# Rotary partners fetched by transfers, the layer norm's sums two chunks sooner, the delta gates on GpSimd, and two row turns held to norms

## The chip, the core and the metric

The kernel runs on one core of a Trainium2 chip. A core has a matmul engine (TensorE, PE in the profile), a vector engine (VectorE, DVE), an activation engine (ScalarE, ACT), a general engine (GpSimd, POOL) and one that here only issues transfers (SyncE, SP); each works through its own list of instructions and waits for the others by semaphores. They share the on-chip memory SBUF; matmuls write to PSUM, eight banks of 2 KB a partition. The metric is device time in microseconds (us) of one launch.

## The reference

Everything is fp32, 256 tokens, width 1024. Two blocks follow one another. Block one has two hybrid layers; block two (norms modulated by a condition vector, latent attention beside a Hyena convolution, SwiGLU) is touched here by one row turn only. Cut to what the change meets:

```python
def hybrid_layer(x, ...):                    # twice
    h = rms_norm(x, norm_w)
    aq, ak, av, az, c_glu, cz, dq, dk, dv, dz, db, da, gates = split(h @ w_in)
    # diff attention: 8 heads, two 64-wide halves each
    q, k = apply_rope(aq), apply_rope(ak)    # [t1*cos - t2*sin, t2*cos + t1*sin]
    p = softmax(q k^T / 8 + causal);  a = p[0] - lam * p[1];  y_a = (rms(a v) * silu(az)) @ w_o
    # conformer convolution
    u = causal_conv31(a_half * sigmoid(g_half)) + b
    y_c = (silu(layer_norm(u)) * silu(cz)) @ w_conv_out
    # gated delta rule: 8 heads of 128, chunks of 64 tokens
    q, k, v = silu(causal_conv4([dq, dk, dv]));  q, k = l2_normalize(q), l2_normalize(k)
    beta = sigmoid(db);  g = -exp(a_log) * softplus(da + dt_bias);  g = cumsum(g)
    y_d = (rms(delta_rule(q, k, v, g, beta)) * silu(dz)) @ w_dn_out
    return x + (s_a * y_a + s_c * y_c + s_d * y_d) @ w_out      # s = sigmoid(gates)
```

apply_rope needs, for each row d of a 64-wide half, its partner row 32 further up or down, once with the sign turned. softplus is worked out as max(a, 0) + ln(1 + exp(−|a|)), with a correction of the logarithm for the rounding of 1 + exp(−|a|).

## The kernel before

Activations lie transposed: 128 channels on the partitions, 256 tokens along a row. Weights come as 128x128 tiles in the order of use, 16 to a load of 1 MB, which SyncE issues into a ring of four. Precision is kept by splitting: ScalarE writes the rounded high part of a load (L778), GpSimd the rest (L663, or VectorE where it has time), and TensorE makes three products for each tile, high by high, low by high, high by low (L1948 to L1950). One output tile of 128 channels over 1024 inputs is a "chunk": 8 tiles, 24 products into one of four PSUM banks (pg), which another engine drains. The other four banks (ps) hold everything that isn't a weight product: norms, rotations, scores.

The order of chunks is written out by a function and is the same for all engines. For a layer of block one: ag (16), qk (16), v (8, tokens on the partitions), dn (24, the delta rule's q, k and v before their convolution), cz 0 to 3 with the narrow projection for beta and the decay (BA) between, then the attention loop of 18 steps, into which cz 4 to 7 and c_out 0 to 15 are spread as fillings, then the delta rule, the three output projections with their gates, and w_out. From the order follow tables that the engines share: after which drain a tile may be read, and how far ahead of a chunk its high and low parts are made.

What the change touches, with the lines of the profile. TensorE rotates the pairs of q and k tiles by a constant matrix (rot, L2123): four of the eight behind v3 and v5, four ahead of dn1, dn2, dn5 and dn6; VectorE's rope (L1656 to L1660) multiplies by the tables. VectorE adds the last three taps of the short convolution for each dn chunk (sconv, L1428), with taps of the 31-wide one (L1413) between. The layer norm's channel sum is made by VectorE (L1723) after sconv 16 and 17, added over the partitions by TensorE (L2359) ahead of dn20; ScalarE squares the centered rows after dn23, VectorE sums them (L1731) and TensorE adds them (L2185) ahead of cz1. For the delta gates ScalarE makes exp and ln, VectorE the eight operations of delta_log (L1493 to L1501) in step 0 of the attention loop, TensorE the running sums (L2206) in step 1, VectorE the rest in step 2. GpSimd multiplies cz 4 to 7 into the branch (L689 to L691). PE L2013 is a row turn: a row of modulation values that block two needs is brought onto the partitions. PE L2149 are attention scores, L2179 a head norm's sums.

```python
for part in range(4):                              # TensorE, v
    for tt in range(NT):
        tokens_first("v", l, 2 * part + tt, ...)
    if part in (1, 2):
        rot1(2 * part - 2); rot1(2 * part - 1)
for i in range(24):                                # TensorE, dn
    if i in (1, 2, 5, 6): rot1(ROPES_V + (1, 2, 5, 6).index(i))
    if i in DQ_AT: half_norm(...)                  # DQ_AT = (15, 18)
    if i == LN_MEAN:
        pe.wait_ge(sem("ln_added"), l + 1)         # the mean's matmul
    chunk("dn", l, i, KD, hx, T)
```

## Time and profile before

| | us |
|---|---|
| three runs | 2552.84, 2544.14, 2553.32 |
| median | 2552.84 |
| profiled execution | 2549.82 |
| its span, first to last instruction | 2548.0 |
| TensorE busy | 2484.7 |
| GpSimd, ScalarE, VectorE busy | 1455.7, 1246.3, 1171.3 |

The profile is of one execution. Its mean granted clock of TensorE was 0.993 of full speed. Times of the timeline are from the span's start; in a row, the first number is the start, the second how long the instruction (or the run of xN alike) took, and in brackets stands how long the engine was idle ahead of it and what ended that. Matmuls are pipelined: a product of 256 columns is shown with 0.28 us, but the next one begins 0.12 us later. In the program's names HH and HL are the high and low parts of the normed input, X holds the convolution branch, big the attention's and the delta rule's tiles, ba the delta gates.

### The profile page before, as it was taken

What the parts mean: (1) busy time and instruction counts of PE and PEld (TensorE: products, weight loads), DVE (VectorE), ACT (ScalarE), POOL (GpSimd) and SP (SyncE); (2) the same over time, 40 slices, a digit from 0 to 9 for tenths busy, and PEclk for the clock granted to TensorE, in tenths of its full rate; (3) what the DMA queues carried; (4) which work ended last, traced back from release to release, by engine and by line L of the source; (5) the groups of instructions that cost most, each with busy time, mean ns of one, the idle gap of its engine ahead of it and who ended that gap; (6) DMA issues with size and microseconds to landing.
All of it is one profiled execution on the core that took longest, in us unless ns stands there. A gap on an engine that the chain in (4) does not pass through costs nothing.

```text
span 2548.0 us, 42067 instructions
## 1 busy us (share of the span) xinstructions
PE 2484.7 (98%) x16588; PEld 2170.4 (85%) x16588; DVE 1171.3 (46%) x2176; ACT 1246.3 (49%) x2113; POOL 1455.7 (57%) x835
## 2 busy tenths in 40 slices
PE   7998999999999899999999999999999999999998
PEld 7997989888999788898777877778888878898998
DVE  8896645444878645536415613331101123535144
ACT  6467654355546764436544522443323345636543
POOL 6875746456977664544533343646565546464970
PEclk9999999999999899999999999999999999999999
DMA  6543343345544344335421022232222233235554
GB/s 244 180 167 145 133 166 134 139 175 182 182 173 160 131 156 154 121 137 206 175 83 66 34 83 81 89 116 90 92 99 95 88 116 127 82 140 193 188 182 149
DMA packets 50601, 347.63 MB, mean 136 GB/s; under 512 B 5361, under 2 KB 8689, under 8 KB 8945
## 3 DMA queue, kind: packets, MB, share of 16 engines
q1 hardware_dynamic: 47840, 340.31, 37.1%
q10 hardware_dynamic: 2576, 4.72, 0.6%
q8 instruction: 133, 2.18, 0.3%
q14 instruction: 52, 0.42, 0.1%
HBM read 343.96 MB, written 1.05 MB: 135 GB/s over the span
## 4 chain that ended last, share of the span: by engine, by line
PE 91%; DVE 4%; ACT 3%; issue 1%; POOL 1%; DMA 1%; ACTq 0%; DVEq 0%; SPq 0%; POOLq 0%
PE pg L1948 23%; PE pg L1950 23%; PE pg L1949 23%; PE ps L2266 2%; PE pg L1971 2%; PE ps L2287 2%; PE ps L2285 1%; PE ps L2423 1%; PE ps L2404 1%; PE ps L2117 1%; ACT ring_hi L778 1%; PE ps L2123 1%; PE ps L2092 1%; PE ps L2504 1%; PE ps L2497 1%
## 5 line engine op out<-in xcount | busy, mean ns | idle before, releaser
L663 POOL TENSOR_TENSOR ring_lo<-ring,ring_hi 128x1024 fp32r<-128x1024 f32 (+3 forms) x502 | 1169.9, 2345 | 705.8 <-ACT ring_hi L778 704.8
L1948 PE MATMUL pg<-HH,ring_hi 128*128 128x256 f32 (+1 forms) x3264 | 1038.7, 318 | 8.1 <-POOL ring_lo L663 5.9
L1949 PE MATMUL pg<-HH,ring_lo 128*128 128x256 f32 (+1 forms) x3264 | 992.2, 304 | 0.0
L1950 PE MATMUL pg<-HL,ring_hi 128*128 128x256 f32 (+1 forms) x3008 | 920.0, 306 | 0.0
L1948 PEld LDWEIGHTS pg<-HH,ring_hi 128*128 128x128 f32 x3264 | 619.2, 190 | 73.8 <-issue 36.9
L1949 PEld LDWEIGHTS pg<-HH,ring_lo 128*128 128x128 f32 x3264 | 619.4, 190 | 43.4 <-issue 16.5
L1950 PEld LDWEIGHTS pg<-HL,ring_hi 128*128 128x128 f32 x3008 | 570.5, 190 | 28.3
L778 ACT ACTIVATE ring_hi<-ring 128x1024 fp32r<-128x1024 f32 (+3 forms) x572 | 563.8, 1003 | 30.3 <-DMA ring<-in_w_stream_dram 22.3
L788 ACT ACTIVATE take<-pg 128x256 f32<-128x256 f32 (+1 forms) x242 | 103.7, 429 | 452.6 <-PE pg L1950 445.0
L1950 PE MATMUL pg<-big_r,ring_hi 128*128 128x256 f32 (+1 forms) x928 | 299.3, 323 | 0.0
L1948 PE MATMUL pg<-big_r,ring_hi 128*128 128x256 f32 (+1 forms) x752 | 246.0, 327 | 3.9 <-DVE ring_lo L1633 2.7
L1949 PE MATMUL pg<-big_r,ring_lo 128*128 128x256 f32 (+1 forms) x752 | 244.1, 325 | 0.0
L1900 DVE TENSOR_TENSOR big_r<-big,big_r 128x512 fp32r<-128x512 f32 (+1 forms) x44 | 58.8, 1336 | 362.7 <-ACT big_r L1253 362.7
L1950 PEld LDWEIGHTS pg<-big_r,ring_hi 128*128 128x128 f32 x928 | 174.5, 188 | 15.3
L1413 DVE SCALAR_TENSOR_TENSOR ps<-big,prm,ps 128x256 f32<-128x256 f32 x464 | 183.6, 489 | 0.0
L788 ACT ACTIVATE big<-pg 128x256 f32<-128x256 f32 (+1 forms) x136 | 59.3, 436 | 232.2 <-PE pg L1950 229.9
L1948 PEld LDWEIGHTS pg<-big_r,ring_hi 128*128 128x128 f32 x752 | 141.4, 188 | 21.2 <-DVE ring_lo L1633 3.3
L1949 PEld LDWEIGHTS pg<-big_r,ring_lo 128*128 128x128 f32 x752 | 141.7, 188 | 13.1 <-issue 0.2
L707 POOL TENSOR_TENSOR X<-X,take 128x256 f32<-128x256 f32 (+1 forms) x50 | 50.4, 1012 | 126.9 <-ACT take L1184 126.9
L1633 DVE TENSOR_TENSOR ring_lo<-ring,ring_hi 128x1024 fp32r<-128x1024 f32 (+3 forms) x70 | 79.8, 1175 | 43.1 <-ACT ring_hi L778 43.1
L1184 ACT ACTIVATE take<-pg,mod 128x256 f32<-128x256 f32 x58 | 25.1, 471 | 145.0 <-PE pg L1950 145.0
L1612 DVE TENSOR_TENSOR big<-big,ps 128x512 f32<-128x512 f32 x40 | 27.5, 688 | 136.8 <-PE ps L2287 136.8
(350 smaller groups left out, 3337.7 us busy)
## 6 DMA issues: line engine op xcount, KB each, us to landing
ring<-in_w_stream_dram SPq DMA_DIRECT2D x320, 1024.0 KB, 4.8
hn<-in_consts_dram ACTq DMA_DIRECT2D x2, 1024.0 KB, 6.0
cst<-in_consts_dram SPq DMA_DIRECT2D x1, 1472.0 KB, 19.5
prm<-in_params_dram SPq DMA_DIRECT2D x1, 1110.0 KB, 9.3
X<-in_xT_dram SPq DMA_DIRECT2D x1, 1024.0 KB, 5.8
X<-in_ctxT_dram ACTq DMA_DIRECT2D x1, 1024.0 KB, 5.9
out_dram<-H ACTq DMA_DIRECT2D x4, 256.0 KB, 2.2
cst<-in_consts_dram SPq DMA_DIRECT2D x1, 768.0 KB, 16.5
```

The source lines that it names most:

```text
L663: pool.tensor_tensor(ring_lo[:, slot, cols], ring[:, slot, cols], ring_hi[:, place * P:(place + n) * P].bitcast(F32), SUB).then_inc(sem(LO ...
L778: act.activation(ring_hi[:, place * P:(place + n) * P], ring[:, slot, cols], ACT.Copy)\
L788: act.activation(dst, ready(j)[:, 0:n], func, scale=scale).then_inc(sem("drained"), 1)
L1413: ins = dve.scalar_tensor_tensor(acc if t < CONV_K - 1 else CV[:, k, :], U[:, k, t:t + T], PR("conv_dw_w", w), acc, MUL, ADD)
L1633: dve.tensor_tensor(ring_lo[:, slot, cols], ring[:, slot, cols], ring_hi[:, place * P:(place + n) * P].bitcast(F32), SUB).then_inc(sem(LOW ...
L1900: dve.tensor_tensor(AFL[l][:, c, :], AF[l][:, c, :], AFH[l][:, c, :].bitcast(F32), SUB).then_inc(sem("af_low"), 1)
L1948: first = pe.matmul(out, a[0], b[0], start=start, stop=False)
L1949: pe.matmul(out, a[1], b[0], start=False, stop=False)
L1950: return first, pe.matmul(out, a[0], b[1], start=False, stop=stop)
L1971: ins = pe.matmul(pg[part, j % 4, :], sc[:, c, :], tile(4), start=c < MOD_TILES, stop=c >= k - MOD_TILES)
L2266: ins = pe.matmul(ps[:, 1, s], LM[v % 2][:, s], TM[:, s], start=True, stop=True)
L2287: ins = pe.matmul(ps[:, 2, s], XS[:, s], TT[:, s], start=True, stop=True)
```

## The change

1. The rotation matmuls of block one are gone. ScalarE issues four transfers from SBUF to SBUF of 32 partitions x 2048 floats (256 KB each) for the first half of the qk tiles after draining qk8, four for the second after v0; they bring the partner rows into two spare buffers. ScalarE then copies each pair of tiles (128x512) to the PSUM bank where the rotation's result stood: two copies after v3, two after v5, one each after dn1, 2, 5 and 6. The sign lies in the sine table.
2. LN_MEAN goes from 20 to 18, so that the mean's matmul stands ahead of dn18. The square is made ahead of dn22's copy and its sum on VectorE ahead of sconv 22, instead of both behind dn23.
3. delta_log is made by GpSimd, in nine operations of 128x16, right behind cz4's products; the reciprocal is replaced by exp(−ln) on ScalarE. The running sums become a chunk of their own ("decay") in a bank of pg in step 7 of the loop, drained by ScalarE, and VectorE's rest moves from step 2 to step 8.
4. The row turn of "do" 0 goes from layer 0's gates into the norm of layer 1, and that of norm 5 from ahead of a k chunk of block two into norm 6.

```diff
@@ -80 +74 @@
-    c["inv1"] = np.tile(inv1, 4)[:, None]
+    c["inv1"] = np.concatenate([-inv1, inv1, -inv1, inv1])[:, None]
@@ -173,0 +168 @@
+LATE_TURNS = {1: ("do", 0), 6: ("norm", 5)}
@@ -184 +179,6 @@
-    return {"before": [("part", x) for x in rows[:1]] * 2, "after": rows, "turns": [("modt", *x[1:]) for x in rows]}[side]
+    late = [("modt", *x) for x in MOD_AT.get(LATE_TURNS.get(i), [])]
+    turns = [] if ("norm", i) in LATE_TURNS.values() else [("modt", *x[1:]) for x in rows]
+    return {"before": [("part", x) for x in rows[:1]] * 2, "after": rows + late, "turns": turns}[side]
+DECAY_STEP = 7
@@ -188 +188,3 @@
-    return spread([("cz", l, m) for m in range(EARLY_CZ, KD)] + [("c_out", l, i) for i in range(2 * KD)], ATT_STEPS + LAG + 1)
+    fills = spread([("cz", l, m) for m in range(EARLY_CZ, KD)] + [("c_out", l, i) for i in range(2 * KD)], ATT_STEPS + LAG + 1)
+    fills[DECAY_STEP].append(("decay", l, 0))
+    return fills
@@ -235 +237 @@
-    return gates[:2] + [row] + gates[2:4] + [turn] + gates[4:]
+    return gates[:2] + [row] + gates[2:4] + ([turn] if l else []) + gates[4:]
@@ -533 +535,0 @@
-        GCS = ps[:, 3, 288:304].rearrange("p (c h) -> p c h", c=NT)
@@ -589 +591,2 @@
-        LN_MEAN = 20
+        LN_MEAN = 18
+        LN_SQUARE = 22
@@ -692,0 +696,12 @@
+            def delta_log(l):
+                pool.wait_ge(sem("over_abs"), l + 1)
+                link(pool.tensor_scalar(NGC, B1, 1.0, None, ADD))
+                link(pool.tensor_scalar(NGC, NGC, -1.0, None, ADD))
+                link(pool.tensor_tensor(NGC, B1, NGC, SUB))
+                link(pool.tensor_tensor(NGC, NGC, GC, MUL))
+                link(pool.tensor_tensor(B2, B2, NGC, ADD))
+                link(pool.tensor_scalar(B0, B0, 0.0, None, MAX))
+                link(pool.tensor_tensor(B0, B0, B2, ADD))
+                link(pool.tensor_tensor(B0, B0, rep(EXA, NT), MUL))
+                pool.tensor_scalar(G, B0, -1.0, None, MUL).then_inc(sem("g_done"), 1)
@@ -721,0 +737,2 @@
+                    if m == EARLY_CZ:
+                        delta_log(l)
@@ -898,0 +918,16 @@
+            def turn_qk(l, half):
+                act.wait_ge(sem("drained"), DRAINED["qk", l, 8 * half + 7])
+                for a, b in ((0, 32), (32, 0), (64, 96), (96, 64)):
+                    act.dma_start(QK_TURNED[half][a:a + 32, :], big[b:b + 32, 2048 * half:2048 * (half + 1)])\
+                        .then_inc(sem(f"qk_turned{half}"), 16)
+            def turned_to_psum(l, jj):
+                i = 8 * l + jj
+                act.wait_ge(sem(f"qk_turned{jj // 4}"), 64 * (l + 1))
+                if i >= 2:
+                    act.wait_ge(sem("rope"), i - 1)
+                act.activation(ps[:, 2 + i % 2, :], QK_TURNED[jj // 4][:, jj % 4 * 2 * T:(jj % 4 + 1) * 2 * T], ACT.Copy)\
+                    .then_inc(sem("turned"), 1)
@@ -966,0 +1002,2 @@
+                act.wait_ge(sem("ln_abs"), l + 1)
+                act.activation(GC, B2, ACT.Exp, scale=-1.0).then_inc(sem("over_abs"), 1)
@@ -969,2 +1006,3 @@
-                act.wait_ge(sem("gc_ready"), l + 1)
-                act.activation(BEG, GCS, ACT.Exp).then_inc(sem("exp_gc"), 1)
+                sums = ready(CHUNK["decay", l, 0])[:, 0:2 * HEADS].rearrange("p (c h) -> p c h", c=NT)
+                act.activation(BEG, sums, ACT.Exp)
+                act.activation(NGC, sums, ACT.Copy, scale=-1.0).then_inc(sem("drained"), 1)
@@ -1048,0 +1087,2 @@
+                    if j == 8:
+                        turn_qk(l, 0)
@@ -1050,0 +1091,5 @@
+                    if j == 0:
+                        turn_qk(l, 1)
+                    if j in (3, 5):
+                        turned_to_psum(l, j - 3)
+                        turned_to_psum(l, j - 2)
@@ -1060,0 +1106,3 @@
+                    if j == LN_SQUARE:
+                        act.wait_ge(sem("ln_centered"), l + 1)
+                        act.activation(hn.rearrange("p (a b) -> p a b", a=KD), CV, ACT.Square).then_inc(sem("ln_sq"), 1)
@@ -1062,0 +1111,2 @@
+                    if j in TURNS_DN:
+                        turned_to_psum(l, ROPES_V + TURNS_DN.index(j))
@@ -1072,2 +1121,0 @@
-                act.wait_ge(sem("ln_centered"), l + 1)
-                act.activation(hn.rearrange("p (a b) -> p a b", a=KD), CV, ACT.Square).then_inc(sem("ln_sq"), 1)
@@ -1490,13 +1536,0 @@
-            def delta_log(l):
-                dve.wait_ge(sem("ln_abs"), l + 1)
-                link(dve.tensor_scalar(GC, B1, 1.0, None, ADD))
-                link(dve.tensor_scalar(NGC, GC, -1.0, None, ADD))
-                link(dve.tensor_tensor(NGC, B1, NGC, SUB))
-                link(dve.reciprocal(GC, GC))
-                link(dve.tensor_tensor(NGC, NGC, GC, MUL))
-                link(dve.tensor_tensor(B2, B2, NGC, ADD))
-                link(dve.scalar_tensor_tensor(B0, B0, 0.0, B2, MAX, ADD))
-                dve.wait_ge(sem("exp_a"), l + 1)
-                dve.scalar_tensor_tensor(G, B0, -1.0, rep(EXA, NT), MUL, MUL).then_inc(sem("g_done"), 1)
@@ -1504,2 +1538 @@
-                dve.wait_ge(sem("exp_gc"), l + 1)
-                dve.wait_ge(sem("beta"), l + 1)
+                dve.wait_ge(sem("drained"), DRAINED["decay", l, 0])
@@ -1507 +1539,0 @@
-                link(dve.tensor_scalar(NGC, GCS, -1.0, None, MUL))
@@ -1655 +1687,4 @@
-                dve.wait_ge(sem("rot"), i + 1)
+                if i < ROPE2[0]:
+                    dve.wait_ge(sem("turned"), i + 1)
+                else:
+                    dve.wait_ge(sem("rot"), i + 1 - ROPE2[0])
@@ -1710,0 +1746,3 @@
+                    if j == LN_SQUARE:
+                        dve.wait_ge(sem("ln_sq"), l + 1)
+                        dve.tensor_reduce(rstd[:, T:2 * T], hn.rearrange("p (m t) -> p t m", m=KD), AX.X, ADD).then_inc(sem("ln_sq_added"), 1)
@@ -1730,2 +1767,0 @@
-                dve.wait_ge(sem("ln_sq"), l + 1)
-                dve.tensor_reduce(rstd[:, T:2 * T], hn.rearrange("p (m t) -> p t m", m=KD), AX.X, ADD).then_inc(sem("ln_sq_added"), 1)
@@ -1752,3 +1788 @@
-                    if it == 0:
-                        delta_log(l)
-                    if it == GATES_AT + 1:
+                    if it == DECAY_STEP + 1:
@@ -2203,0 +2240,5 @@
+                j = CHUNK["decay", l, 0]
+                assert j == at["chunk"]
+                at["chunk"] += 1
+                bank_free(j)
@@ -2206,2 +2247,2 @@
-                    ins = pe.matmul(GCS[:, c, :], C("until"), G[:, c, :], start=True, stop=True)
-                ins.then_inc(sem("gc_ready"), 1)
+                    ins = pe.matmul(pg[:, j % 4, HEADS * c:HEADS * (c + 1)], C("until"), G[:, c, :], start=True, stop=True)
+                ins.then_inc(sem("chunk_ready"), 1)
@@ -2336 +2376,0 @@
-                rot1 = lambda jj: rot(8 * l + jj, C("rot1"), QK[:, 2 * jj:2 * jj + 2, :])
@@ -2342,8 +2381,0 @@
-                    if part == 1:
-                        pe.wait_ge(sem("drained"), DRAINED["qk", l, 15])
-                        if l == 0:
-                            pe.wait_ge(sem("rope_table"), 1)
-                            pe.wait_ge(sem("tables"), 32)
-                    if part in (1, 2):
-                        rot1(2 * part - 2)
-                        rot1(2 * part - 1)
@@ -2351,2 +2382,0 @@
-                    if i in (1, 2, 5, 6):
-                        rot1(ROPES_V + (1, 2, 5, 6).index(i))
@@ -2372 +2400,2 @@
-                        pe.wait_ge(sem("gates_done"), l + 1)
+                        pe.wait_ge(sem("abs_a"), l + 1)
+                        pe.wait_ge(sem("beta"), l + 1)
```

Left out are the decay chunk's entries in the tables and the lists of gates, which follow the row turn.

TensorE at the layer norm's mean, before; L2359 is the mean's matmul, ln_added the end of VectorE's sum, and the three products ahead of it belong to dn19:

```order
L1948 MATMUL pg<-HH,ring_hi 128x256
L1949 MATMUL pg<-HH,ring_lo 128x256
L1950 MATMUL pg<-HL,ring_hi 128x256
L2359 MATMUL ps<-rstd,cst 128x256 [waits ln_added]
L1948 MATMUL pg<-HH,ring_hi 128x256 [waits low_ready,sconv]
L1949 MATMUL pg<-HH,ring_lo 128x256
```

And after; the same matmul is L2389, L2215 are the sums of the q norm, and the products that follow belong to dn18:

```order
L1984 MATMUL pg<-HL,ring_hi 128x256
L2215 MATMUL ps<-H,cst 128x512 [waits hn_done,hn_sq]
L2215 MATMUL ps<-H,cst 128x512
L2389 MATMUL ps<-rstd,cst 128x256 [waits ln_added]
L1982 MATMUL pg<-HH,ring_hi 128x256 [waits low_ready,sconv]
L1983 MATMUL pg<-HH,ring_lo 128x256
```

The matmul moved ahead by two chunks, 48 products, and stands right behind the q norm's sums.

GpSimd at the first cz products of the attention loop, before; L689 to L691 are the products, L663 the low parts:

```order
L689 TENSOR_TENSOR HH<-X,take 128x256 [waits cz_double]
L690 TENSOR_TENSOR X<-X,take 128x256
L691 TENSOR_TENSOR XL<-X,HH 128x256 [waits pool_link]
L663 TENSOR_TENSOR ring_lo<-ring,ring_hi 128x1024 [waits high_ready]
L689 TENSOR_TENSOR HH<-X,take 128x256 [waits cz_double]
```

And after (L692 to L694 the products, L666 the low parts, L698 to L706 delta_log):

```order
L694 TENSOR_TENSOR XL<-X,HH 128x256 [waits pool_link]
L698 TENSOR_SCALAR ba<-ba 128x16 [waits over_abs]
L699 TENSOR_SCALAR ba<-ba 128x16 [waits pool_link]
L700 TENSOR_TENSOR ba<-ba 128x16 [waits pool_link]
L701 TENSOR_TENSOR ba<-ba 128x16 [waits pool_link]
L702 TENSOR_TENSOR ba<-ba 128x16 [waits pool_link]
L703 TENSOR_SCALAR ba<-ba 128x16 [waits pool_link]
L704 TENSOR_TENSOR ba<-ba 128x16 [waits pool_link]
L705 TENSOR_TENSOR ba<-ba 128x16 [waits pool_link]
L706 TENSOR_SCALAR ba<-ba 128x16 [waits pool_link]
L666 TENSOR_TENSOR ring_lo<-ring,ring_hi 128x1024 [waits high_ready]
```

Nine linked operations stand between cz4's last product and the next low parts.

ScalarE in the v chunks after the change; L805 drains v chunks, L795 makes high parts, L922 issues the transfers, L931 copies to PSUM:

```order
L805 ACTIVATE big<-pg 128x256 [waits chunk_ready]
L922 DMA at_buf<-big 32x2048 [waits drained]
L922 DMA at_buf<-big 32x2048 x3
L805 ACTIVATE big<-pg 128x256 [waits chunk_ready]
L795 ACTIVATE ring_hi<-ring 128x1024 [waits chunk_ready,weights2] x2
L805 ACTIVATE big<-pg 128x256 [waits chunk_ready] x2
L931 ACTIVATE ps<-hn 128x512 [waits qk_turned0] x2
L795 ACTIVATE ring_hi<-ring 128x1024 [waits chunk_ready,weights3] x2
L805 ACTIVATE big<-pg 128x256 [waits chunk_ready] x2
```

Two copies now stand between v3's drain and the high parts of the next load, which followed the drain directly.

## Rows read from the trace of the kernel before

**Rows 1.** The page: busy time by engine, share, instructions.

```profile
PE 2484.7 (98%) x16588; PEld 2170.4 (85%) x16588; DVE 1171.3 (46%) x2176; ACT 1246.3 (49%) x2113; POOL 1455.7 (57%) x835
...
```

**Rows 2.** TensorE's waits, whole span: us in total, times, longest.

```profile
PE ps L2185 <- DVE rstd L1731: 6.6, 2, 3.3
...
PE ps L2206 <- DVE ba L1501: 4.3, 2, 2.2
PE ps L2149 <- DVE at_buf L1456: 3.3, 2, 1.8
...
```

**Rows 3.** Timeline, v chunks: start, us, engine, line, operation, count, idle before.

```profile
119.27 4.75 POOL L663 TENSOR_TENSOR ring_lo<-ring,ring_hi 128x1024 fp32r<-128x1024 f32 x2 [3.20 <-ACT ring_hi L778]
...
123.26 1.88 PE L2123 MATMUL ps<-big,cst 128*128 128x512 f32 x4
...
124.86 5.23 POOL L663 TENSOR_TENSOR ring_lo<-ring,ring_hi 128x1024 fp32r<-128x1024 f32 x2 [0.84 <-ACT ring_hi L778]
...
125.09 0.28 PE L1949 MATMUL pg<-ring_hi,HL 128*128 128x256 f32 x1
...
131.71 0.69 DVE L1656 TENSOR_TENSOR at_buf<-big,cst 128x512 f32<-128x512 f32 x1 [2.55 <-PE ps L2123]
...
```

**Rows 4.** Timeline, layer 0, dn4 to dn6.

```profile
154.02 2.42 DVE L1428 SCALAR_TENSOR_TENSOR big<-pg,prm,big 128x255 f32<-128x255 f32 x6
...
157.50 1.02 PE L2123 MATMUL ps<-big,cst 128*128 128x512 f32 x2
...
158.48 0.28 PE L1949 MATMUL pg<-HH,ring_lo 128*128 128x256 f32 x1
...
```

**Rows 5.** Timeline, layer 0, dn18 to cz1.

```profile
196.45 0.68 PE L1948 MATMUL pg<-HH,ring_hi 128*128 128x256 f32 x1
...
198.06 3.94 DVE L1723 TENSOR_REDUCE rstd<-X 128x256 f32<-128x2048 f32 x1
...
202.53 0.59 PE L2359 MATMUL ps<-rstd,cst 128*128 128x256 f32 x2
...
222.35 0.70 PE L2185 MATMUL ps<-rstd,cst 128*128 128x256 f32 x2 [3.32 <-DVE rstd L1731]
...
```

**Rows 6.** Windows: us, busy PE PEld DVE ACT POOL, PEclk, DMA, GB/s.

```profile
223.80:227.10 3.30, 3.30 (x18) 3.30 (x17) 2.29 (x1) 2.05 (x4) 3.30 (x2) 0.50 0.00 0
832.50:838.10 5.60, 5.60 (x24) 5.42 (x25) 3.35 (x2) 3.48 (x5) 4.71 (x2) 0.50 0.02 3
...
```

**Rows 7.** Timeline, layer 0, attention loop with cz5 to c_out1.

```profile
248.28 2.21 DVE L1499 SCALAR_TENSOR_TENSOR ba<-ba 128x16 f32<-128x16 f32 x1
...
250.52 0.17 DVE L1501 SCALAR_TENSOR_TENSOR ba<-ba 128x16 f32<-128x16 f32 x1
...
250.75 0.75 PE L2206 MATMUL ps<-ba,cst 128*128 128x8 f32 x4 [2.17 <-DVE ba L1501]
...
253.52 0.73 POOL L689 TENSOR_TENSOR HH<-X,take 128x256 fp32r<-128x256 f32 x1 [3.07 <-DVE take L1481]
...
267.84 0.75 POOL L690 TENSOR_TENSOR X<-X,take 128x256 f32<-128x256 f32 x1
...
268.67 0.73 POOL L691 TENSOR_TENSOR XL<-X,HH 128x256 fp32r<-128x256 f32 x1
...
270.23 0.28 PE L1948 MATMUL pg<-HH,ring_hi 128*128 128x256 f32 x1
```

**Rows 8.** Groups by shape: busy us, mean ns of one, idle before.

```profile
L814 ACT ACTIVATE mod_rows<-pg 128x512 f32<-128x512 f32 x24 | 14.1, 587 | 14.4 <-PE pg L1971 14.4
...
L663 POOL TENSOR_TENSOR ring_lo<-ring,ring_hi 128x128 fp32r<-128x128 f32 x4 | 1.9, 469 | 0.0
...
```

**Rows 9.** Timeline: a DMA queued by ScalarE.

```profile
1215.20 0.61 ACTq L1145 DMA_DIRECT2D X<-in_ctxT_dram  x1
...
```

**Rows 10.** Timeline: the row turn of norm 5; norm 6.

```profile
1723.45 0.95 PE L2013 MATMUL pg<-cst,mod_rows 128*128 128x2 f32 x8
...
2344.77 0.39 PE L1994 MATMUL pg<-HH,ring_hi 128*128 128x256 f32 x1 [3.21 <-ACT HH L908]
...
```

More of the change, by code:

```diff
@@ L58, in constants @@
     c["levels"] = np.concatenate(lv, 1)
-    rot1 = np.zeros((P, P))
-    for d in range(P):
-        if d % QK_DIM < QK_DIM // 2:
-            rot1[d + QK_DIM // 2, d] = -1.0
-        else:
-            rot1[d - QK_DIM // 2, d] = 1.0
-    c["rot1"] = rot1
+    c["spare"] = np.zeros((P, P))
     c["tab1"] = np.zeros((P, 2 * T))
@@ L107, in constants @@
     return c
-CONST_W = {"until": P, "later": P, "causal1": T, "levels": 7 * P, "rot1": P, "tab1": 2 * T,
+CONST_W = {"until": P, "later": P, "causal1": T, "levels": 7 * P, "spare": P, "tab1": 2 * T,
            "ident": P, "ones": P, "eps6": 1, "eps5": 1, "half_pi": 1, "lam_init": DEPTH, "inv1": 1, "sel": 2,
@@ L330, in n_tiles @@
         return KH
-    return {"down": KF // FF_PARTS[l], "mod": 4 * KD, "modt": 0}.get(name, KD)
+    return {"down": KF // FF_PARTS[l], "mod": 4 * KD, "modt": 0, "decay": 0}.get(name, KD)
 def is_split(name, l, i):
-    return name not in ("mod", "modt")
+    return name not in ("mod", "modt", "decay")
 def vector_splits(name, l, i):
@@ L509, in build @@
         MG = H[:, :, T:2 * T]
+        QK_TURNED = [hn[:, :], sq]
         AT_S = cut(at_buf, 0, 2, 2 * T)
@@ L587, in build @@
         ROPES_V = 4
+        TURNS_DN = (1, 2, 5, 6)
         CONV_EARLY = 12
-        LN_MEAN = 20
+        LN_MEAN = 18
+        LN_SQUARE = 22
         DQ_AT = (15, 18)
@@ L833, in drain_fill @@
                         hyena_in(l, i)
+                    elif name == "decay":
+                        delta_decay(l)
                     else:
@@ L1117, in _ @@
                 hn_root(HN_BASE1(l) + DO_N, 2048, 1.0 / P)
-                drain_fill(gates[1:6])
+                middle = gates.index(("d_out", l, KD))
+                drain_fill(gates[1:middle])
                 for m in range(KD):
@@ L1125, in _ @@
                     if m == KD // 2 - 1:
-                        drain_fill(gates[6:7])
+                        drain_fill(gates[middle:middle + 1])
                 if l == DEPTH - 1:
                     filter_sin(0, 0)
-                drain_fill(gates[7:])
+                drain_fill(gates[middle + 1:])
                 if l == DEPTH - 1:
@@ L2031, in fill @@
                         turn_rows(*item[1:])
+                    elif item[0] == "decay":
+                        delta_decay(item[1])
                     else:
```

7 lines of the change are left out of this document (1 added, 6 removed).

## Prediction

> **What bounds the kernel now.** I began with the page's busy times: TensorE is busy for 2484.7 of 2548.0 us, 98% of the span, and no other engine for more than 57% [rows 1]. So only two things can move the end much: work that leaves TensorE, and TensorE's waits. I then read the list of TensorE's waits, then the timeline around each place that the diff touches, in layer 0 (layer 1 of block one repeats it some 610 us later), and last the clock by windows. The waits that the change aims at are small: 6.6 us at the layer norm's second sum, 4.3 at the delta gates' running sums, 3.3 at the attention turn behind them, each over two layers [rows 2]. The profiled execution took 2549.8 us, 1.8 more than its span and 3.0 under the median of the three runs (2552.8); I sum against 2549.8.
>
> **The rotary partners: what leaves TensorE.** Two rotations in a row stand between v chunks. From the start of the pair at 123.26 to the second product of the next chunk at 125.09 there are 1.83 us, and one product takes 0.12, so a pair costs 1.71 [rows 3]. One rotation alone costs 158.48 − 157.50 − 0.12 = 0.86 [rows 4]. Per layer 2 × 1.71 + 4 × 0.86 = 6.9 us, 13.7 in both.
>
> **What is late next.** Chunk v4 cannot start before GpSimd has split its weights into low parts. That split starts at 119.27 and ends at 124.02 [rows 3]; v4's first product now starts about 125.0, so of the first 1.71 only about 0.8 comes in. The split for v6 runs 124.86 to 130.09; it waits for ScalarE's high parts, in front of which ScalarE now has two copies of 128x512 to PSUM. Such a copy takes 0.59 us [rows 8], two 1.2, so that split ends near 131.3. v7 thus ends some 0.95 us sooner, not 3.4. The eight DMAs per layer are queued by ScalarE at about 0.61 us each [rows 9]: 2.4 us per half, in a stretch where it does no more per chunk than one copy and two high parts, and the partners of the first half are wanted 20 us later. I cost them at nothing; if that cover were gone they would delay the high parts by 2.4 us twice. Their 2 MB lie beside the weight stream, and no wait of TensorE on weights stands in this stage.
>
> The rope of pair 2 on VectorE follows v5 and starts near 131.0 instead of 131.71 [rows 3]. From there VectorE works without idle time up to 181, so everything in this stretch moves by 0.7 to 1.0 us and no more. The dn chunks share PSUM banks with VectorE's short convolution: dn6 needs the convolution of chunk 2. That pair of convolutions runs 154.02 to 156.4 [rows 4], from now on about 1.0 sooner, to 155.4. TensorE would be ready for dn6 at 158.36 − 0.95 − 4 × 0.86 = 154.0, so it waits 1.4. At dn10 the same happens again. TensorE leaves dn14 about 1.1 us sooner: of 6.9 us, 5.8 have turned into waits.
>
> **The layer norm's mean before dn18.** Now dn18 starts at 196.45, and VectorE's sum over the eight channel tiles runs 198.06 to 202.0; the mean's matmul at 202.53 finds it done, because dn18 and dn19 lie between [rows 5]. After the change this matmul stands ahead of dn18. VectorE still has its convolution and two taps in front of the sum, so the sum ends at 202.0 − 1.1 = 200.9, while TensorE is ready at about 195.3. It stands still for 5.6 us, with dn18, dn19 and the k norm queued behind it, and dn18 starts at 201.1, 4.65 later than now. In return the wait of 3.32 us at 222.35 [rows 5] goes: the square is made before dn22's copy and the sum lies two chunks sooner.
>
> **The clock.** The rows show what such a wait brings with it. After the 3.32 us wait the granted clock stood at 0.50 (1.2 GHz) from 223.8 to 227.1, and in layer 1, after the same wait, for 5.6 us from 832.5 on [rows 6]. Work at half clock takes double, so a dip costs 1.65 or 2.8 us; for one whose length I cannot see I take their mean, 2.2. The Trainium skill ("TensorE: Matmul & The Clock Gate", Why this matters for your kernels) warns against idle gaps of TensorE between bursts; the rows above agree, and by that rule the longer wait ahead of dn18 would have its dip too.
>
> Up to cz2: 4.65 + 2.2 (dip) − 0.3 (the mean's matmul, no longer ahead of dn20) − 3.3 − 1.65 (the old wait's dip) = +1.6.
>
> **delta_log on GpSimd.** On VectorE the chain ends with 2.21 us for one 128x16 operation [rows 7]; TensorE then waits 2.17 for the running sums at 250.75 and 1.8 more for the turn [rows 2, 7]. Both go, with 0.2 of the sums: −4.1. But the nine operations now stand on GpSimd between the products of cz4 and the split and products of cz5 to cz7, and a chain without idle time there leads to the last row at 268.67, done 269.40; TensorE uses it at 270.23 [rows 7]. From cz4's first row at 253.52 to the end are 15.9 us. No row shows GpSimd on 16 columns. Its split of 128 columns takes 0.469 us [rows 8], one of 1024 columns 4.75 / 2 = 2.38 [rows 3], so 2.1 ns a column and 0.23 us at 16 columns. A link costs 268.67 − 267.84 − 0.75 = 0.08 [rows 7]. Nine operations and eight links: 2.7 us. Bounds: nine times the 0.17 that VectorE takes for its last one of these [rows 7], 1.5 us; and nine times the 0.73 of a 256-column row plus links, 7.2. I take 2.7, which comes from the nearest rows of GpSimd. The Trainium skill ("GPSIMD Engine Reference", 3.1 Elementwise — side-by-side cycle accounting) has GpSimd 1.96 times slower than VectorE on one elementwise operation at a width of 2048; an estimate by that page from 0.17 us is 9 × 0.33 = 3.0 us, 0.3 more for each layer's sum than mine; no run here shows the factor at 16 columns.
>
> cz4's rows start at 253.52 + 1.6 − 3.0 = 252.1 (of the 4.1, 3.0 lie ahead of them). So cz7's last row is done at 252.1 + 15.9 + 2.7 = 270.7, where TensorE now asks for it at 270.23: +0.5. TensorE itself comes some 5 us early, waits there, and pays a dip, +2.2. Layer 0: **+2.7**. In layer 1 the kernel before loses (5.6 − 3.3) / 2 = 1.15 more to its dip [rows 6], which goes with the wait: +1.55. Adding up, 13.7 us of rotations and 14.2 us of named waits leave nothing, since their ends are set by VectorE up to the mean and by GpSimd up to cz7.
>
> **The two row turns.** One turn takes 0.95 us, 0.8 net, on TensorE [rows 10]. That of norm 5 goes into norm 6's wait of 3.21 us for ScalarE [rows 10]: −0.8. That of "do" goes into norm 1's wait, but where it stood the next chunk waits for its low parts anyway: 0.
>
> Sum: 2549.8 + 2.7 + 1.55 − 0.8 = **2553.3 us**.
>
> **Rivals.** A: TensorE's work and waits simply add up. The 98% speaks for it, and also that every removed wait is named by the change. 13.7 + 6.6 + 4.3 + 3.3 + 0.8 = 28.7 us less: 2521 us. Against it: VectorE without idle time from 131.7 to 181, the 202.0 at the end of the sum, and the end at 269.40 on GpSimd. It could be partly true if VectorE's chain gets shorter where GpSimd competes less with it.
> B, slower: narrow operations on GpSimd cost as much as wide ones (0.73 and a link). The delta_log of 7.2 us then delays cz7's rows by 4.5 us more in each layer; it decides from 2.2 us on (2.7 less the 0.5), where the slack is used up and TensorE gets each further one as a wait at c_out1. 2553.3 + 9.0 = 2562.3 us. For it: the one 2.21 us row of VectorE for 16 columns beside GpSimd, which shows that narrow operations in this place can be dear. Against it: 0.469 us at 128 columns.
> C: the new waits are followed by no dip. Then each layer gains twice 2.2 on the forecast: 2553.3 − 8.8 = 2544.5 us. Against it: a dip followed the 3.3 us wait in both layers.
>
> **How the numbers follow.** Forecast 0.50 (with its own range of 2545 to 2558, which is one dip more or fewer per layer and 2 us on the GpSimd chain), A or a good part of it 0.20, B 0.18, C 0.12. What can be told from no change is about 0.5%, 12.7 us. A lies beyond it, and with it a small part of C: faster 0.22. B ends at 2562.3, near the bound of 2562.5, and in the upper part of it goes over: slower 0.13. The rest, 0.65, is within. The range leaves out the far part of A and little above B: 2533 to 2564.
>
> **What would show it.** Right: no L2123 rows in block one; waits of TensorE for low parts at v6 and for the short convolution at dn6 and dn10, together over 2 us; ahead of dn18 a wait of 5 to 6 us for the sum, with a clock of 0.50 behind it; no wait at the second sum; nine GpSimd rows of 0.2 to 0.3 us, and a wait of some 5 us for GpSimd within c_out1. Wrong: a wait ahead of dn18 under 3 us (the VectorE chain was shorter than read), GpSimd rows of 0.5 us or more (B), a clock of 1.0 behind both waits (C), or layer distances that fall by over 8 us (A).

## The result: slower by 0.8%

The changed kernel takes 2571.56 us (median, 2570.84 to 2572.32) against 2550.23 us of the kernel before on the same chip: ratio 1.0083, 95% interval 1.0065 to 1.0100. The profiled execution has a span of 2569.1 us, 21.1 more than before. From the page of the changed kernel (busy time by engine; the chain that ended last; two groups of DMA issues with KB each and us to landing):

```profile
PE 2479.8 (97%) x16556; PEld 2171.1 (85%) x16556; DVE 1164.0 (45%) x2158; ACT 1255.9 (49%) x2133; POOL 1460.3 (57%) x853
...
PE 84%; DVE 6%; ACT 4%; POOL 3%; DMA 1%; issue 1%; ACTq 0%; DVEq 0%; SPq 0%; POOLq 0%
...
hn<-big ACTq DMA_DIRECT2D x8, 256.0 KB, 5.2
at_buf<-big ACTq DMA_DIRECT2D x8, 256.0 KB, 4.9
```

TensorE is busy for 4.9 us less than in [rows 1] and idles 26 us more; its share of the chain fell from 91% to 84%. The rotations that left are 13.7 us of work. Some 8.8 us of busy time thus came back, and the clock is the likely reason: within the span it was granted at 0.50 for 54.8 us, in the kernel before for 37.2, and half of the 17.6 us between them is 8.8. TensorE's waits, as in [rows 2] (us in total, times, longest):

```profile
PE pg L1982 <- POOL ring_lo L666: 11.1, 14, 2.2
...
PE ps L2389 <- DVE rstd L1761: 9.5, 2, 4.7
PE pg L2028 <- ACT HH L950: 8.5, 2, 6.1
PE pg L1982 <- DVE big L1475: 7.8, 4, 3.5
PE pg L1982 <- POOL XL L694: 7.7, 2, 3.9
PE pg L2028 <- ACT HH L943: 6.4, 1, 6.4
...
PE ps L2185 <- DVE at_buf L1503: 2.1, 4, 1.0
```

The three waits of [rows 2] are gone or down to 2.1 us, and in their place stand a wait for VectorE's sum ahead of dn18 (9.5), for the short convolution (7.8), for GpSimd's products of cz7 (7.7), and the waits at the norms, 6.07 and 6.4 us where they were 2.9 and 3.2. Of the two old ones, that of norm 6 is in [rows 10]; norm 1 is the longest wait of this line of the kernel before:

```profile
PE pg L1994 <- ACT HH L915: 5.4, 2, 2.9
```

Where the time went is seen best by the start of the same product in both timelines (us from the span's start; in layer 1 everything lies 610 us later):

| chunk | before | after | difference |
|---|---|---|---|
| dn3 | 148.12 | 145.46 | −2.7 |
| dn7 | 161.20 | 162.78 | +1.6 |
| dn18 | 196.45 | 204.10 | +7.7 |
| cz2 | 230.91 | 233.99 | +3.1 |
| c_out1 | 267.64 | 267.02 | −0.6 |
| c_out6 | 287.78 | 293.71 | +5.9 |
| ag2, layer 1 (behind norm 1) | 636.90 | 645.22 | +8.3 |
| c_out6, layer 1 | 898.87 | 914.65 | +15.8 |
| first chunk behind norm 6 | 2353.08 | 2374.15 | +21.1 |

Up to the end of layer 0 the difference is 5.7 us, norm 1 adds 2.6, layer 1 adds 7.6, the stretch up to norm 6 adds 0.2 and norm 6 adds 5.0.

The v and dn stretch. In the kernel before, ScalarE drains v1 here:

```profile
117.86 0.38 ACT L788 ACTIVATE big<-pg 128x256 f32<-128x256 f32 x1 [2.42 <-PE pg L1950]
```

In the changed kernel: ScalarE's queueing of four transfers and the same drain, rope products of VectorE (L1691) beside GpSimd's splits (L666), and dn6's wait for the convolution:

```profile
115.05 3.65 ACTq L922 DMA_DIRECT2D at_buf<-big  x4
118.74 0.38 ACT L805 ACTIVATE big<-pg 128x256 f32<-128x256 f32 x1 [3.31 <-PE pg L1984]
...
124.35 1.08 DVE L1691 TENSOR_TENSOR at_buf<-big,cst 128x512 f32<-128x512 f32 x1 [8.95 <-ACT ps L931]
...
126.79 2.04 DVE L1691 TENSOR_TENSOR at_buf<-big,cst 128x512 f32<-128x512 f32 x1
...
128.76 0.69 DVE L1693 TENSOR_TENSOR ps<-ps,cst 128x512 f32<-128x512 f32 x1
...
131.84 0.69 DVE L1691 TENSOR_TENSOR at_buf<-big,cst 128x512 f32<-128x512 f32 x1 [1.67 <-ACT ps L931]
...
128.24 2.86 POOL L666 TENSOR_TENSOR ring_lo<-ring,ring_hi 128x1024 fp32r<-128x1024 f32 x1
...
133.31 5.22 POOL L666 TENSOR_TENSOR ring_lo<-ring,ring_hi 128x1024 fp32r<-128x1024 f32 x2 [2.21 <-ACT ring_hi L795]
...
133.90 2.37 DVE L1691 TENSOR_TENSOR at_buf<-big,cst 128x512 f32<-128x512 f32 x1
...
152.03 5.15 POOL L666 TENSOR_TENSOR ring_lo<-ring,ring_hi 128x1024 fp32r<-128x1024 f32 x2 [1.62 <-ACT ring_hi L795]
...
152.32 2.65 DVE L1691 TENSOR_TENSOR at_buf<-big,cst 128x512 f32<-128x512 f32 x1
...
156.23 2.42 DVE L1475 SCALAR_TENSOR_TENSOR big<-pg,prm,big 128x255 f32<-128x255 f32 x6
...
158.32 0.39 PE L1982 MATMUL pg<-HH,ring_hi 128*128 128x256 f32 x1 [3.26 <-DVE big L1475]
```

The four transfers hold ScalarE's queue until 118.70. v1's last product ended as early as before, but its drain starts 0.88 us later, and with it come the high parts and the low parts behind it: v4 waits 1.57 us for them.

Alone the rope's first product takes 0.69 us. Where a split of GpSimd is already running, it ends 0.54 to 0.56 us behind the end of that split, in all six such ropes of layer 0 before and all six after the change. It lasted 1.20 to 1.90 us so before, and 1.08 to 2.66 after. Over the eight ropes of layer 0 this line sums to 13.8 us instead of 10.8. The rope of pair 2 also starts no sooner than in [rows 3] (131.84 against 131.71), because it waits for ScalarE's copy. The convolutions of dn2 and dn3 now end at 158.6, not at 156.4 as in [rows 4], and dn6 waits 3.26 us.

The layer norm's mean (answering to [rows 5]): VectorE's sum and the matmul that waited 4.75 us for it. The second sum's matmul, at 227.06, now has no wait.

```profile
199.75 3.64 DVE L1761 TENSOR_REDUCE rstd<-X 128x256 f32<-128x2048 f32 x1
...
203.44 1.22 PE L2389 MATMUL ps<-rstd,cst 128*128 128x256 f32 x2 [4.75 <-DVE rstd L1761]
```

The attention loop, GpSimd, answering to [rows 7]: cz4's first product, the first and the last of the nine operations of delta_log, the split behind them, cz7's last product and TensorE's wait for it:

```profile
254.98 0.75 POOL L692 TENSOR_TENSOR HH<-X,take 128x256 fp32r<-128x256 f32 x1
...
257.21 0.27 POOL L698 TENSOR_SCALAR ba<-ba 128x16 f32<-128x16 f32 x1
...
259.74 0.26 POOL L706 TENSOR_SCALAR ba<-ba 128x16 f32<-128x16 f32 x1
259.96 2.38 POOL L666 TENSOR_TENSOR ring_lo<-ring,ring_hi 128x1024 fp32r<-128x1024 f32 x1
...
272.85 0.72 POOL L694 TENSOR_TENSOR XL<-X,HH 128x256 fp32r<-128x256 f32 x1
...
273.62 0.39 PE L1982 MATMUL pg<-HH,ring_hi 128*128 128x256 f32 x1 [3.85 <-POOL XL L694]
```

From 257.21 to 259.96 the nine operations take 2.75 us. Clock by windows, as in [rows 6]:

```profile
158.95:162.30 3.35, 3.35 (x18) 3.35 (x18) 3.35 (x10) 1.10 (x2) 2.17 (x1) 0.50 0.68 232
203.30:206.70 3.40, 3.26 (x13) 3.08 (x14) 0.09 (x1) 0.00 (x0) 0.95 (x1) 0.50 0.15 19
275.00:278.40 3.40, 3.40 (x17) 3.36 (x16) 2.12 (x7) 1.83 (x6) 3.40 (x3) 0.50 0.42 116
2360.60:2370.70 10.10, 5.70 (x26) 5.71 (x27) 6.39 (x16) 8.46 (x16) 3.03 (x3) 0.50 0.48 179
```

With each of the three new waits of layer 0 come 3.4 us at 0.50 of the full clock (1.2 GHz), 10.2 us together, as much as the kernel before had in this layer (3.4 and 6.8 us). In layer 1 it is 20.4 us where it was 13.6. Norm 6's wait brings 10 us of it, which begin 4.5 us before the wait ends. With its old wait of 3.2 us came none in the profiled execution of the kernel before, and 3.4 us in those of experiments 1, 9 and 12, where the wait is the same.

And norm 1. In the kernel before, the table load for the root stands right behind two high parts (622.37 to 624.36):

```profile
624.37 1.28 ACT L856 ACT_TABLE_LOAD   x1
```

In the changed kernel: ScalarE's high parts, SyncE's loads, ScalarE's third high part, the root, and TensorE's wait:

```profile
628.07 1.99 ACT L795 ACTIVATE ring_hi<-ring 128x1024 fp32r<-128x1024 f32 x2
...
628.40 10.05 SPq L634 DMA_DIRECT2D ring<-in_w_stream_dram  x3
...
633.12 1.06 ACT L795 ACTIVATE ring_hi<-ring 128x1024 fp32r<-128x1024 f32 x1 [3.07 <-DMA ring<-in_w_stream_dram]
...
635.49 0.45 ACT L880 ACTIVATE ps<-ps,cst 128x256 f32<-128x256 f32 x1
...
637.36 0.58 PE L2028 MATMUL pg<-HH,ring_hi 128*128 128x256 f32 x1 [6.07 <-ACT HH L950]
```

Between the norm's sum and its root stands a high part (633.12) for which ScalarE waits 3 us until its load has landed. SyncE issued that load, the first of its three, at 628.40, and it was there 4.7 us later, which is usual: the page's median for these loads of 1 MB is 4.8 us.

The turn of norm 5 stood in another place than [rows 10] have it. The row at 1723.45 is the turn of norm 4, and it is still there after the change, at 1739.65. The turn that moved, in the kernel before:

```profile
2104.57 0.95 PE L2013 MATMUL pg<-cst,mod_rows 128*128 128x2 f32 x8
```

And the first product behind its old place, in the changed kernel:

```profile
2121.44 0.36 PE L1982 MATMUL pg<-HH,ring_hi 128*128 128x256 f32 x1 [0.52 <-POOL ring_lo L666]
```

With the turn gone TensorE waits for low parts there, and the difference to the kernel before falls by 0.1 us only (16.2 to 16.1). The turn of "do" 0 gave 0.2 us where it stood.

### The profile page after: what moved, and what is told of

It is laid out like the page before. It is cut to its first block, busy times and chain, and to the rows that moved or that the text cites. A ratio compares the mean times of both kernels' runs of the same rounds, so it can differ in the third digit from the quotient of the medians.

```text
span 2569.1 us, 42051 instructions
## 1 busy us (share of the span) xinstructions
PE 2479.8 (97%) x16556; PEld 2171.1 (85%) x16556; DVE 1164.0 (45%) x2158; ACT 1255.9 (49%) x2133; POOL 1460.3 (57%) x853
## 4 chain that ended last, share of the span: by engine, by line
PE 84%; DVE 6%; ACT 4%; POOL 3%; DMA 1%; issue 1%; ACTq 0%; DVEq 0%; SPq 0%; POOLq 0%
PE pg L1982 22%; PE pg L1983 21%; PE pg L1984 21%; PE ps L2307 2%; PE ps L2328 2%; PE pg L2005 2%; POOL ring_lo L666 2%; PE ps L2326 1%; PE ps L2452 1%; PE ps L2433 1%; PE ps L2153 1%; DMA ring<-in_w_stream_dram 1%; ACT ring_hi L795 1%; DVE ps L1460 1%; PE ps L2533 1%
## 5 line engine op out<-in xcount | busy, mean ns | idle before, releaser
L666 POOL TENSOR_TENSOR ring_lo<-ring,ring_hi 128x1024 fp32r<-128x1024 f32 (+3 forms) x502 | 1168.1, 2342 | 725.1 <-ACT ring_hi L795 724.3
L795 ACT ACTIVATE ring_hi<-ring 128x1024 fp32r<-128x1024 f32 (+3 forms) x572 | 564.0, 1002 | 46.2 <-DMA ring<-in_w_stream_dram 28.9
L805 ACT ACTIVATE take<-pg 128x256 f32<-128x256 f32 (+1 forms) x242 | 103.8, 429 | 456.6 <-PE pg L1984 449.6
L805 ACT ACTIVATE big<-pg 128x256 f32<-128x256 f32 (+1 forms) x136 | 59.2, 435 | 222.3 <-PE pg L1984 218.3
L1983 PEld LDWEIGHTS pg<-big_r,ring_lo 128*128 128x128 f32 x752 | 142.0, 189 | 13.1 <-issue 0.2
```

Source lines behind the costliest of these rows:

```text
L666: pool.tensor_tensor(ring_lo[:, slot, cols], ring[:, slot, cols], ring_hi[:, place * P:(place + n) * P].bitcast(F32), SUB).then_inc(sem(LO ...
L795: act.activation(ring_hi[:, place * P:(place + n) * P], ring[:, slot, cols], ACT.Copy)\
L805: act.activation(dst, ready(j)[:, 0:n], func, scale=scale).then_inc(sem("drained"), 1)
L1983: pe.matmul(out, a[1], b[0], start=False, stop=False)
```

## Experiments

Every experiment is shown with its edit against the changed kernel or the one named. Measured: the median of the kernel and its ratio to the kernel before, which was run beside it; its medians were 2549.58 us for experiments 1 to 4, 2548.64 for 5 to 8 and 2548.53 for 9 to 12. Experiments 9 to 12 ran on another chip than 1 to 8, so where one of them is compared with experiment 8, the ratios with their intervals count.

**1. The row turns back.**

```diff
-LATE_TURNS = {1: ("do", 0), 6: ("norm", 5)}
+LATE_TURNS = {}
```

(and the turn of "do" 0 back in its list).

> The changed kernel with its two row turns put back where they were (part 4 undone, all else as changed). Theory M: the changed kernel loses at norm 1 and norm 6 because ScalarE, ahead of the norm's root, now makes one high part more, whose load has not landed (3.1 us of waiting each, and a clock dip behind norm 6): this kernel should be 7 to 9 us under the changed one (2571.6), near 2563, with waits of 2.9 to 3.2 us at both norms. Rival R1: the loss comes from block one's two layers alone and the turns cost nothing: within 2 us of the changed kernel.

Measured 2565.58 us, ratio 1.0065 [1.0046, 1.0084]: 6.0 us less than the changed kernel, somewhat under the 7 to 9 expected. The waits at the norms are again 2.9 and 3.2 us. R1, which left no more than 2 us, falls.

**2. The high part behind the root.**

```diff
-                    ahead(CHUNK[NORM_USER[i]] - 1, ...)
+                    ahead(CHUNK[NORM_USER[i]] - (2 if i in LATE_TURNS else 1), ...)
```

> The changed kernel, turns as changed, but ScalarE makes high parts only up to one step less ahead of the roots of norms 1 and 6, so that the third high part comes behind the root. Theory M: that high part and its load are the cause, not the turn: 7 to 9 us under the changed kernel, as with the turns put back, or up to 1 us better. Rival R2: the turn's matmuls and the wait for its row (0.9 us each) are the cost: no more than 2 us gained.

Measured 2564.97 us, 1.0066 [1.0046, 1.0085]: 6.6 us less, again a little under the 7 to 9. ScalarE at norm 1, its high parts, the root, and TensorE's wait:

```profile
628.92 1.99 ACT L795 ACTIVATE ring_hi<-ring 128x1024 fp32r<-128x1024 f32 x2
...
632.22 0.45 ACT L880 ACTIVATE ps<-ps,cst 128x256 f32<-128x256 f32 x1
...
634.08 0.58 PE L2028 MATMUL pg<-HH,ring_hi 128*128 128x256 f32 x1 [1.95 <-ACT HH L950]
```

The turns are where the change put them, and the loss is gone. So the turn itself costs nothing that can be told; it counts as a step in the order of chunks, and the rule "high parts up to one step ahead of the norm's user" thereby reached one high part further. R2 falls.

**3. The mean ahead of dn20 again.**

```diff
-        LN_MEAN = 18
+        LN_MEAN = 20
```

> The changed kernel with the mean's matmul ahead of dn20 again (the square stays ahead of dn22's copy). Theory M: the wait of 4.7 us ahead of dn18 and its dip go in both layers and come back only in part, as a wait at the k norm or at the second sum: 5 to 9 us under the changed kernel. Rival R3: VectorE's chain sets the end wherever the matmul stands, so the wait only moves: within 2 us of the changed kernel.

Measured 2557.52 us, 1.0038 [1.0026, 1.0051]: 14.0 us less, more than expected. TensorE's wait for the second sum comes back with 0.5 us in each layer only, not with 3.3, since the square is still made early. R3 falls.

**4. The rotations back on TensorE**, with the sign back in the matrix and the transfers and copies taken out.

```diff
-                    if j == 8:
-                        turn_qk(l, 0)
...
+                    if part in (1, 2):
+                        rot1(2 * part - 2)
+                        rot1(2 * part - 1)
...
+                    if i in (1, 2, 5, 6):
+                        rot1(ROPES_V + (1, 2, 5, 6).index(i))
```

> The changed kernel with the rotations of block one back on TensorE (part 1 undone, all else as changed). Theory M: the rotary partners by transfer and copy saved no time, since VectorE's chain got 2.2 us longer per layer in its ropes and dn6 then waits 3.3 us plus a dip: without it the kernel is 2 to 8 us faster than the changed one, with rope rows of VectorE as before. Rival R4: TensorE's work counts, and its return costs what it takes: 6 to 13 us slower than the changed kernel.

Measured 2572.57 us, 1.0092 [1.0072, 1.0111]: no difference to the changed kernel that can be told. 13.7 us of work returned to TensorE and cost nothing. Both theories miss: the kernel is not 2 to 8 us faster and not 6 to 13 slower. The waits:

```profile
PE ps L2394 <- DVE rstd L1755: 9.5, 2, 4.8
PE pg L1976 <- POOL XL L700: 7.7, 2, 3.9
```

The wait for dn6's convolution is gone, and the mean's wait is 9.5 us in both kernels. As it ends when VectorE's sum does, it may take up what TensorE gains or loses ahead of it; experiments 5 and 6 take it away.

**5 and 6. Both repairs; and with them the rotations on TensorE.** The edits of 2 and 3 together, then those of 4 on top:

```diff
-                    ahead(CHUNK[NORM_USER[i]] - 1, ...)
+                    ahead(CHUNK[NORM_USER[i]] - (2 if i in LATE_TURNS else 1), ...)
...
-        LN_MEAN = 18
+        LN_MEAN = 20
```

> The changed kernel with the high part behind the roots of norms 1 and 6, and with the mean's matmul ahead of dn20. Theory M: the two repairs touch different places, so their gains add up: 2571.6 - 6.6 - 14.0 = 2551 us, within 2. Rival R5: a part of the 14.0 was clock or a change further on that the first repair takes as well: 2554 or more.

Measured 2551.32 us, 1.0009 [0.9999, 1.0019], as added up; R5 falls. The two repairs take back 20.2 of the 21.3 us that the changed kernel had lost by the medians.

> The same with the rotations of block one back on TensorE. With the mean ahead of dn18 their return cost nothing (2572.6 against 2571.6), perhaps only because the wait for the mean took it up. Theory M: it is the ropes' longer time on VectorE, then the wait ahead of dn6 and its dip, which eat the 6.9 us per layer wherever the mean stands: within 3 us of the kernel of this call with the partners by transfer. Rival R6: the wait for the mean hid the gain; with it gone the rotations on TensorE cost 6 to 12 us more.

Measured 2546.93 us, 0.9993 [0.9983, 1.0002]: TensorE's rotations are 4.4 us faster than the transfers and copies, with intervals that barely overlap. Neither theory had this right, a draw within 3 us or a cost of 6 to 12 us: with the mean's wait gone, part 1 is a loss.

**7. The copies as soon as the partners are there.** On 5:

```diff
+                    if j == 13:
+                        turned_to_psum(l, 0)
+                        turned_to_psum(l, 1)
+                turn_qk(l, 1)
...
-                    if j in (3, 5):
-                        turned_to_psum(l, j - 3)
-                        turned_to_psum(l, j - 2)
+                    if j in (1, 2, 3, 4, 5, 6):
+                        turned_to_psum(l, j + 1)
...
-        ROPES_V = 4
+        ROPES_V = 8
```

(the copies behind dn chunks go, VectorE's ropes between the convolutions give way to taps).

> Partners by transfer, both repairs, and ScalarE copies the turned pairs to PSUM as soon as they are there (two behind qk13, one behind each of v1 to v6; the second half's transfers ahead of v0's drain), so that VectorE does all eight ropes before the dn chunks, in the 8.9 us in which it idled. Theory M: VectorE's lateness at dn6 was the cause of that wait; wait and dip go, 4 to 6 us per layer: near 2541 (2538 to 2544). Rival R7: the low parts, or VectorE's short convolutions themselves, keep the dn chunks at their pace: over 2547.

Measured 2542.38 us, 0.9977 [0.9967, 0.9987]: 8.9 us less than 5, and 4.6 less than 6 with TensorE's rotations. Of TensorE's waits:

```profile
PE pg L1977 <- POOL XL L694: 7.7, 2, 3.9
...
PE pg L1977 <- DVE big L1474: 1.8, 2, 1.3
```

The wait for the convolution fell from 8.0 us in experiment 5 to 1.8, and R7 falls. So VectorE's lateness ahead of dn6 was what ate the rotations' 6.9 us per layer.

**8. delta_log behind cz7.** On 7:

```diff
-DECAY_STEP = 7
+DECAY_STEP = 13
...
                     times_z("cz", l, m, CV, CVH, CVL)
-                    if m == EARLY_CZ:
-                        delta_log(l)
+                delta_log(l)
```

> The same, and GpSimd makes delta_log behind the last product of cz7 instead of behind cz4's; the running sums' chunk goes from step 7 to step 13. Theory M: its 2.7 us leave the chain that c_out1 waits for, so the wait of 3.9 us there falls to about 1.1 and its dip goes: 2.7 to 4.5 us per layer less than the kernel before it, near 2533. Rival R8: c_out1's wait is set by when cz4's product starts and by the low parts, so nothing or under 1 us per layer comes back.

Measured 2534.46 us, 0.9940 [0.9924, 0.9957]: 7.9 us less.

```profile
PE pg L1976 <- POOL XL L694: 3.8, 2, 1.9
...
PE pg L1976 <- DVE big L1473: 2.0, 2, 1.2
```

c_out1 waits 1.9 us a layer for GpSimd instead of 3.9, though 2.7 left its chain; about 1.1 had been expected. R8 falls.

**9. On 8, the turns back** (edit of 1).

> The best kernel so far (partners early, mean ahead of dn20, delta_log behind cz7, 2534.5 us) with the two row turns back in their old places. Theory M: with the high part kept behind the root, the late turns are worth what the waits took in, 0.8 us at norm 6 and up to 1 at norm 1: this kernel 0.5 to 2 us slower, near 2535.5. Rival R9: behind the norm the turns cost as much as before: no difference that can be measured.

Measured 2532.13 us, 0.9942 [0.9928, 0.9955]. It is 2.3 us faster than 8 by the medians, and the ratios do not differ. So the late turns are worth nothing that can be told even when repaired, as R9 said; the 0.5 to 2 us expected did not show.

**10. On 8, square and second sum behind dn23.** ScalarE's lines and VectorE's alike:

```diff
-                    if j == LN_SQUARE:
-                        act.wait_ge(sem("ln_centered"), l + 1)
-                        act.activation(hn..., CV, ACT.Square).then_inc(sem("ln_sq"), 1)
...
+                act.wait_ge(sem("ln_centered"), l + 1)
+                act.activation(hn..., CV, ACT.Square).then_inc(sem("ln_sq"), 1)
                 half_root(DK_N, 0)
```

> The best kernel so far, but the square and its sum behind dn23 again, as before the change. Theory M: the wait of 3.3 us at the second sum comes back in both layers with its dip (1.65 and 2.8 us): 8 to 11 us slower, near 2544. Rival R10: VectorE has run ahead through the early ropes, so the wait is small: under 4 us slower.

Measured 2543.53 us, 0.9981 [0.9972, 0.9990]: 9.1 us slower than 8, as expected, with intervals of the ratios that do not touch. The wait at the second sum is back:

```profile
PE ps L2213 <- DVE rstd L1759: 6.6, 2, 3.3
```

**11. On 8, delta_log on VectorE in step 10**, with ScalarE's exp(−ln) for the reciprocal:

```diff
-                delta_log(l)                    # GpSimd, behind cz7
...
+                    if it == 10:
+                        delta_log(l)            # VectorE
```

> The best kernel so far, with delta_log back on VectorE in seven operations, but in step 10 of the attention loop, since the running sums are wanted only in step 13. Theory M: what made VectorE the wrong engine was step 0, not VectorE: the 1.9 us of waiting for GpSimd at c_out1 shrink and nothing new appears: 1 to 4 us faster, near 2532. Rival R11: VectorE's narrow operations beside GpSimd's take the 3.7 us they took and TensorE waits for the attention weights instead: 2 or more us slower.

Measured 2536.86 us, 0.9953 [0.9939, 0.9967], 2.4 us slower than 8 by the medians, but the intervals overlap. The gain of 1 to 4 us did not come, and this theory falls: the wait for GpSimd stayed and the attention scores (L2178) wait longer for VectorE, as R11 has it.

```profile
PE ps L2178 <- DVE at_buf L1488: 4.7, 4, 1.4
...
PE pg L1975 <- POOL XL L694: 3.9, 2, 1.9
```

In 8 the wait for VectorE was 1.9 us in total. GpSimd's last cz product, not what stands behind it, sets c_out1's wait.

**12. The kernel before with part 2's square and second sum alone.** The edit of 10 the other way round, on the kernel before:

```diff
+        LN_SQUARE = 22
...
+                    if j == LN_SQUARE:
+                        dve.wait_ge(sem("ln_sq"), l + 1)
+                        dve.tensor_reduce(rstd[:, T:2 * T], ...).then_inc(sem("ln_sq_added"), 1)
```

> The kernel before with one edit alone: square ahead of dn22's copy and its sum ahead of sconv 22; the mean stays ahead of dn20, rotations, delta gates and turns as before. Theory M: this edit carries the gain of the whole change: the wait of 3.3 us at the second sum goes in both layers with its dips: 6 to 10 us faster than the kernel before (2548.6), near 2541. Rival R12: VectorE then comes later to the delta gates or to cz's products, so it gives under 3 us.

Measured 2543.58 us, 0.9977 [0.9968, 0.9986]: 5.0 us faster than before, a little under the 6 to 10 expected; R12 falls. It is a gain that needs nothing else of the change. What is left of the wait of 6.6 us in [rows 2]:

```profile
PE ps L2188 <- DVE rstd L1715: 0.9, 2, 0.5
```

Versions 8 and 9 beat both kernels: 0.6% under the kernel before, 1.4 to 1.5% under the changed one.

## Why the prediction was wrong

The forecast was 2553.3 us, the range up to 2564; measured were 2571.6. The profiled execution took 2570.8 us, 17.5 more than the sum. About 8.4 of them are one step, the row turns; 9.1 lie in the two layers of block one (13.3 measured, 4.25 forecast).

- *The row turns* ("goes into norm 6's wait: −0.8", and 0 for the other). This step failed as a whole. I looked for idle time of TensorE to put the turn in, and found it. I did not follow what ScalarE does ahead of the root, whose reach is counted in steps of the order, and the turn is one. Measured: +2.6 us at norm 1 and +5.0 at norm 6 with its dip, 7.6 instead of −0.8; experiment 2 gives 6.6 of them back. The −0.8 was wrong by itself too: I had read the row of norm 4's turn for that of norm 5, and at its true place the turn gave 0.1 us.
- *The low parts at v4 and v6.* TensorE waited there, 1.6 and 0.4 us, and dn0 starts 0.95 us sooner, as forecast.
- *Transfers queued by ScalarE at no cost.* Four took 3.65 us, 0.9 each and not 0.61, and the cover that I had counted on was short by 0.9 us: v1's drain came that much later, and so did v4's low parts. By v6 this is absorbed, since the split there ends at 131.1, as forecast.
- *VectorE moves 0.7 to 1.0 us sooner* failed in sign. The rope of pair 2 did not start sooner, since it waited for ScalarE's copy, and the first products of three ropes up to dn2's convolution took 2.1 us longer, each under a split of GpSimd. VectorE came 2.2 us later. dn6 waited 3.3 us, not 1.4, and a dip of 1.7 followed; dn10 waited for nothing. Forecast was a gain of 1.1 us a layer from the rotations; experiments 5 and 6 show a loss of 4.4 over both. Experiments 5 to 7 show the cause: VectorE's lateness. That it comes from the overlap with splits is read from the rows; no run took the splits away.
- *The mean ahead of dn18*: mechanism right, wait 4.75 for 5.6 us, but the sum ended at 203.4, not 200.9, because of the step before. The dip was there, 3.4 us at half clock, so 1.7 for 2.2. It was the dearest part of the change, and the forecast had it so: its terms come to 4.65 + 2.2 − 0.3, 13.1 us over both layers, and experiment 3 gives 14.0. Up to cz2 +3.1 instead of +1.6, because of the start.
- *The square and its sum two chunks sooner.* The wait and its dips stood in the sum with 11.0 us over both layers. Between dn23 and cz2 of layer 0 the timeline gained 5.1 us, as forecast (4.95). To the end it was worth 5.0 us on the kernel before (experiment 12) and 9.1 on that of experiment 8 (experiment 10); what takes the rest back further on stays open.
- *delta_log on GpSimd*: 2.75 us for 2.7, and from cz4's first product to cz7's last 18.6 us for 15.9 + 2.7. But the chain started at 255.0, not 252.1: GpSimd had a split of 2.4 us in front of it, and everything ahead was late. c_out1's wait was 3.85 us, and the layer ended at +5.9 instead of +2.7. The sum also leaves out the 6.8 us at half clock that the kernel before had at the delta gates' wait in each layer (251.1 and 862.1), which went.
- *Layer 1*: I gave it 1.15 less than layer 0, on the ground that its old dips go. They went, but longer ones came, 20.4 us at half clock for 13.6: from +8.3 to +15.9.

A, B and C all missed. B had the sign and the place (c_out1), not the cause: narrow operations on GpSimd are cheap.

## What to carry to other kernels

Where an engine's look-ahead is counted in steps of a shared order, adding an empty step changes what the other engines do; after moving an item, read all engines' order there, not only that of the engine with the idle time. An engine that is 46% busy can still be the one that sets the time in a stretch. Work taken off the engine that bounds the kernel is worth nothing until its neighbour is earlier too. Here the same partners, fetched by the same transfers, became a gain once VectorE could take them in the 9 us in which it had idled. And an operand wanted late should be made late: delta_log in front of cz5 cost 7.9 us more than behind cz7.
